# A new order of the pair loop, an earlier first expert transfer, and the first transposed inverse by TensorE's transposes

## The reference

```python
proj = rmsnorm(x) @ w_in                       # 2048 -> 3360 (RWKV) + 4096 (retention)
# RWKV-7, per head and step:
sa = einsum('hvk,hk->hv', S, -kk)
S = S * w + sa[..., None] * b + v[..., None] * k
y = einsum('hvk,hk->hv', S, r)
# then a norm of y per head, a bonus term and a gate
# retention, per head and chunk of 128:
o = ((q @ k.T) * decay) @ v + (q @ R) * decay_q
# then a norm and silu(gate)
x = x + concat(y_a, y_b) @ w_out
x = x + moe(rmsnorm(x))                        # top 1 of 4 groups, top 2 of 8 experts
out = rmsnorm(x)
```

## Time and profile before

| | us |
|---|---|
| median of three runs | 2032.34 |
| the profiled execution's own time | 2036.68 |
| its span | 2034.9 |
| PE busy, share of the span | 1682.4, 83% |
| DVE, ACT, POOL busy | 605.2, 279.8, 124.0 |
| pass 0 | 33.7 to 125 |
| pair loop, seven passes | 125 to 900 |
| drain and output projection | 900 to 1068 |
| logits, routing, first gather | 1068 to 1090 |
| experts and stores | 1090 to 2034.9 |

### The profile page before, as it was taken

One profiled execution on the slowest core, in us unless ns is written; L12 is line 12 of the kernel. 1 busy time (PEld: TensorE's weight loads), 2 busy tenths in 40 slices (PEclk: granted clock), 3 DMA queues, 4 the chain that ended last, 5 costly groups with the idle time before them and its releaser, 6 DMA issues.

```text
span 2034.9 us, 25650 instructions
## 1 busy us (share of the span) xinstructions
PE 1682.4 (83%) x9134; PEld 1020.5 (50%) x9134; DVE 605.2 (30%) x1094; ACT 279.8 (14%) x560; POOL 124.0 (6%) x101
## 2 busy tenths in 40 slices
PE   8998999989998989899999758586685857777665
PEld 4776767767776767676666313232231312323111
DVE  6536264545445363632003101111110101111013
ACT  2221222222221212120103000000000000000002
POOL 0201111020202020110000000000000000000000
PEclk9999999999999999999999878797887878878778
DMA  7223222213222232215616999999999999999996
GB/s 280 99 77 112 72 95 76 92 64 105 82 72 90 77 110 76 94 65 170 273 62 283 427 428 428 427 428 428 429 428 429 428 428 428 429 428 429 427 410 244
DMA packets 71041, 510.35 MB, mean 251 GB/s; under 512 B 20401, under 2 KB 23601, under 8 KB 37585
## 3 DMA queue, kind: packets, MB, share of 16 engines
q1 hardware_dynamic: 70944, 509.60, 62.1%
q0 software_dynamic: 48, 0.12, 0.0%
HBM read 499.87 MB, written 9.82 MB: 250 GB/s over the span
## 4 chain that ended last, share of the span: by engine, by line
PE 52%; DMA 32%; DVE 10%; issue 2%; SPq 1%; ACT 1%; DVEq 1%; ACTq 0%
DMA arena<-w_up 21%; PE ps_PJ L641 16%; DMA arena<-w_down 11%; DVE arena L1302 10%; PE ps_C L960 8%; PE ps_PJ L839 7%; PE ps_C L699 2%; PE ps_C L722 1%; SPq L510 1%; ACT arena L1043 1%; PE ps_C L1011 1%; PE ps_SB L1011 1%; PE ps_YB L1011 1%; PE ps_RT L805 1%; PE ps_SB L756 1%
## 5 line engine op out<-in xcount | busy, mean ns | idle before, releaser
L641 PE MATMUL ps_PJ<-arena 128*128 128x320 f32 x1792 | 542.1, 434 | 4.0 <-ACTq L374 4.0
L960 PE MATMUL ps_C<-arena 128*32 128x512 f32 x2048 | 285.1, 720 | 176.6 <-DMA arena<-w_gate 95.8
L641 PEld LDWEIGHTS ps_PJ<-arena 128*128 128x128 f32 x1792 | 319.8, 190 | 111.5 <-issue 11.6
L960 PEld LDWEIGHTS ps_C<-arena 128*32 128x32 f32 x2048 | 80.9, 129 | 374.7 <-issue 372.4
L1302 DVE TENSOR_TENSOR arena<-arena,ps_PJ 128x512 f32<-128x512 f32 (+2 forms) x112 | 73.5, 657 | 572.8 <-PE ps_PJ L936 449.2
L1043 ACT ACTIVATE arena<-ps_C 128x512 f32<-128x512 f32 (+1 forms) x68 | 40.6, 598 | 1064.9 <-PE ps_C L960 594.4
L1302 DVE TENSOR_TENSOR arena<-arena 128x320 f32<-128x320 f32 (+12 forms) x238 | 161.4, 678 | 47.5 <-ACTq L374 25.8
L1780 POOL TENSOR_TENSOR arena<-arena 128x640 f32<-128x640 f32 (+2 forms) x80 | 118.2, 1478 | 780.5 <-DVEq L374 423.1
L839 PE MATMUL ps_PJ<-arena 128*128 128x320 f32 x512 | 145.8, 437 | 2.1 <-DVEq L374 2.1
L929 PE MATMUL ps_PJ<-arena 128*128 128x128 f32 (+1 forms) x768 | 136.2, 308 | 0.0
L929 PEld LDWEIGHTS ps_PJ<-arena 128*128 128x128 f32 (+1 forms) x768 | 104.4, 188 | 40.8 <-issue 11.7
(11 more groups left out here) (183 smaller groups left out, 1364.0 us busy)
## 6 DMA issues: line engine op xcount, KB each, us to landing
arena<-w_gate SPq DMA_DIRECT2D x64, 2048.0 KB, 20.1
arena<-w_up SPq DMA_DIRECT2D x64, 2048.0 KB, 20.9
arena<-w_down SPq DMA_DIRECT2D x64, 2048.0 KB, 20.8
arena<-win SPq DMA_DIRECT2D x59, 1024.0 KB, 4.8
arena<-w_out SPq DMA_DIRECT2D x16, 1024.0 KB, 6.5
arena<-xT SPq DMA_DIRECT2D x8, 640.0 KB, 6.9
arena<-s_ret SPq DMA_DIRECT2D x8, 512.0 KB, 3.8
o_sret<-arena SPq DMA_DIRECT2D x8, 512.0 KB, 4.0
```

Of the source, the lines that this page charges most:

```text
L641: last = mm(pj(j)[:, 0:T], wt[j % NSLOT][:, kt, :], hT[:, kt, :], start=kt == 0, stop=kt == KT - 1)
L960: last = mm((GB, UB)[u][h * CAP:(h + 1) * CAP, :], xg[:, kt, h * CAP:(h + 1) * CAP], w[h][:, k, :], start=kt == 0, stop=kt == KT - 1)
```

## The change

It has five parts. First, `PLAN` and `PLAN0` are new: the retention steps from `sc` to `ms` move from the pass after into their own pass, steps are cut in smaller ones (`pa` into `p1`, `p2`; `pb` into `b1`, `b2a`, `b2b`; `ss` into `sq`, `ss`; `mu` into `my`, `mu`; `pv` into `pr`, `pw`; `ms` into `ms`, `mr`, `mg`; the rotations in two each), and banks and the drain's fill (`LATE`) are set accordingly. Second, `lp` and `ls` transpose the masked `GM` on TensorE, and ScalarE copies the result into `L`; VectorE's two maskings are gone. Third, a new step `u0` transposes `V` of the four chunks on TensorE, and ScalarE copies it into `U`, in place of GpSimd's two products over 640 columns; GpSimd keeps two of 128 columns for the samples. `V` itself is made in two pieces, `v0` and `v1`. Fourth, in the opening of the experts only the first gather stands ahead of the first matmuls, which work on half of the rows (k 0 to 3); then the second gather follows, and the four weight pieces 8 to 11 are fetched in halves (`ex_half`), the first half as soon as those matmuls are done. Fifth, the last logits come ahead of the last transposes, and a sum moves behind the routing's last product.

```diff
-    "C2": ["g2", "du1", "du2", "du3", "du4", "s0", "s1", "s2", "s3", "mu", "va"],
+    "C2": ["g2", "u0", "du1", "du2", "du3", "du4", "s0", "s1", "s2", "s3"],
...
-    "RT": ["tkk", "tvv", "sc", "rt1", "oo", "rt2", "ms", "u1", "u2"],
+    "RT": ["tkk", "sc", "tvv", "rt1", "oo", "rt2", "ms", "u1", "u2", "mu", "va"],
-WARM = [28, 5]
+WARM = [24, 5]
...
-    "k": "-@g -s0 | zw -tvv | -r1 | za -sc | -a1 pc | -rt1 | -s1 | -oo",
-    "r": "-r2 @k | pe -rt2 | -a2 | -ms | -s2 | ss -u1 | -r3 -u2 | -a3 ps",
-    "v": "@r | -s3 | | | -mu pa | pb | -va |",
-    "q": "@v | g0 pd | g1 | g2 | g3 | lp g4 | ls |",
-    "kr": "@q | z1 | zs1 | d1 ds1 | -pv | z2 rq | zs2 | d2 ds2",
-    "vr": "@kr | z3 | tv d3 | rk tb bs | z4 tk | tkk d4 | ts | z5",
-    "g": "@vr gg | rs0 d5 | rs1 | r0 | as | a0 | us |",
+    "k": "-@g -u1 -th | -s1 -mr | zw -u2 | -r2 za -mg | pc | -a2 pe | | -s2",
+    "r": "@k | -r3 | sq | -a3 ss | p1 | -s3 ps | | b1 b2a",
+    "v": "@r | | b2b | -my | -mu | g4 p2 | g0 | g1",
+    "q": "@v v0 g2 -va | g3 v1 | lp ls | u0 | z1 | zs1 pd | | d1 ds1",
+    "kr": "@q | rqa z2 | zs2 | rqb d2 ds2 | | z3 | tv | d3",
+    "vr": "@kr | rka z4 tb | tk | rkb d4 -pr | ts | z5 | tkk -pw | d5",
+    "g": "@vr r0 sc bs | tvv a0 gg | rs0 | s0 rt1 | rs1 oo | r1 rt2 as | ms | a1 us",
...
-    "r": "-r2 @k | -rt2 | -a2 | -ms | zw -s2 | za pc ss -u1 | pe -r3 -u2 | -a3 ps",
+    "k": "| | | | | | |",
+    "r": "@k | | | sq | zw | za pc | ss pe | p1 ps",
+    "v": "@r b1 | b2a | b2b | | | g4 p2 | g0 | g1",
+LATE = {"u1": 1, "s1": 2, "u2": 1, "r2": 2, "a2": 2, "s2": 2, "r3": 2, "a3": 2, "s3": 4, "mu": 5, "va": 5}
...
+            def ex_half(c, half, arrived):
+                s = ESLOT[c % NSLOT_C]
+                dst = arena[:, experts_at + s * BIGSLOT:experts_at + (s + 1) * BIGSLOT].rearrange("p (k n) -> p k n", k=8)
+                src = w_gate[c % QUAD, 2 * F:4 * F, :].rearrange("(p k) n -> p k n", k=8)
+                sp.dma_start(dst[:, 4 * half:4 * half + 4, :], src[:, 4 * half:4 * half + 4, :]).then_inc(arrived, 16)
...
-            for c in range(NSLOT_C, PIECES):
+            sp.wait_ge(sem("half_used"), 1)
+            for c in range(NSLOT_C, NSLOT_C + QUAD):
+                ex_half(c, 0, sem("half_in"))
+            for c in range(NSLOT_C, NSLOT_C + QUAD):
+                sp.wait_ge(ex_used, c - NSLOT_C + 1)
+                ex_half(c, 1, ex_in[ESLOT[c % NSLOT_C]])
...
+                    wait_freed(pe, "g2", p)
+                    wait_freed(pe, "g3", p)
                     for c in range(NC):
-                        last = mm(b[:, c * P:(c + 1) * P], AR[:, c, 0:P], Bd[:, c, :], start=True, stop=True)
+                        last = nc.tensor.transpose(b[:, c * P:(c + 1) * P], GM[:, c, 0:P], ident)
+                    last.then_inc(full(s), 1)
+                elif s == "u0":
+                    wait_done(pe, "inv0v", p)
+                    for c in range(NC):
+                        last = nc.tensor.transpose(b[:, c * P:(c + 1) * P], V[:, c, :], ident)
                     last.then_inc(full(s), 1)
                 elif s == "ls":
-                    mm(b[:, 0:P], AR[:, NC, 0:P], Bd[:, NC, :], start=True, stop=True).then_inc(full(s), 1)
+                    nc.tensor.transpose(b[:, 0:P], GM[:, NC, 0:P], ident).then_inc(full(s), 1)
                 elif s in ("tv", "tb", "tk"):
                     src = {"tv": Vd, "tb": Bd, "tk": Kd_}[s]
...
-                        gather(2 * q + 1, sel0)
-                    pe.wait_ge(named["xg_done"], 4 * it + (4 * q + 2 if opening else 2 * q + 2))
+                        if q == 1:
+                            gather(2 * q + 1, sel0)
+                            if first(it):
+                                pe.wait_ge(sem("half_in"), 16 * QUAD)
+                    if opening and q == 0:
+                        pe.wait_ge(named["xg_done"], 4 * it + 1)
+                    else:
+                        pe.wait_ge(named["xg_done"], 4 * it + (4 * q + 2 if opening else 2 * q + 2))
...
+                            if opening and q + u == 0 and k == 4:
+                                last.then_inc(sem("half_used"), 1)
+                                gather(1, sel0)
+                                pe.wait_ge(named["xg_done"], 4 * it + 2)
...
+                elif s == "lp":
+                    wait_filled(act, s, p)
+                    if not first(p):
+                        act.wait_ge(lmk, 5 * p)
+                    A(L[:, 0:NC, :], bank(s)[:, :].rearrange("p (c n) -> p c n", c=NC), ACT.Copy).then_inc(free(s), 1)
+                elif s == "u0":
+                    wait_filled(act, s, p)
+                    A(U[:, 0:NC, :], bank(s)[:, :].rearrange("p (c n) -> p c n", c=NC), ACT.Copy).then_inc(free(s), 1)
+                elif s == "ls":
+                    wait_filled(act, s, p)
+                    A(L[:, NC, :], bank(s)[:, 0:P], ACT.Copy).then_inc(free(s), 1)
...
+                elif s == "b1":
+                    if not first(p):
+                        wait_filled(dve, "ts", p - 1)
+                    by_heads(Bd, lambda o, h: STT(o, heads(t1)[h], 0.5, heads(ei)[h], ALU.mult, ALU.mult))
+                    by_heads(Kd_, lambda o, h: TT(o, heads(kp)[h], heads(ei)[h], ALU.mult))
+                elif s == "b2a":
                     if not first(p):
                         dve.wait_ge(full("y"), p)
                     by_heads(AR, lambda o, h: STT(o, heads(kn)[h], -1.0, heads(e0)[h], ALU.mult, ALU.mult))
-                    TT(AR[:, :, P:192], heads(xm["r"]), heads(e1), ALU.mult)
-                    by_heads(Bd, lambda o, h: STT(o, heads(t1)[h], 0.5, heads(ei)[h], ALU.mult, ALU.mult))
-                    by_heads(Kd_, lambda o, h: TT(o, heads(kp)[h], heads(ei)[h], ALU.mult)).then_inc(done("bd"), 1)
+                elif s == "b2b":
+                    TT(AR[:, :, P:192], heads(xm["r"]), heads(e1), ALU.mult).then_inc(done("bd"), 1)
                 elif s == "bs":
...
-                elif s == "lp":
-                    wait_filled(dve, s, p)
-                    if not first(p):
-                        dve.wait_ge(lmk, 5 * p)
-                    TT(L[:, 0:NC, :], bank(s)[:, :].rearrange("p (c n) -> p c n", c=NC), lmask[0][:, None, :].broadcast_to([P, NC, P]), ALU.mult).then_inc(free(s), 1)
-                elif s == "ls":
-                    wait_filled(dve, s, p)
-                    TT(L[:, NC, :], bank(s)[:, 0:P], lmask[1], ALU.mult).then_inc(free(s), 1)
-                    wait_freed(dve, "g4", p)
-                    TT(V[:, :, :], GM[:, :, 0:P], m0T[:, None, :].broadcast_to([P, NCH, P]), ALU.mult)
-                    TT(V[:, :, :], V[:, :, :], ident[:, None, :].broadcast_to([P, NCH, P]), ALU.add).then_inc(done("inv0v"), 1)
+                elif s in ("v0", "v1"):
+                    cs = slice(0, 2) if s == "v0" else slice(2, NCH)
+                    nch = cs.stop - cs.start
+                    TT(V[:, cs, :], GM[:, cs, 0:P], m0T[:, None, :].broadcast_to([P, nch, P]), ALU.mult)
+                    last = TT(V[:, cs, :], V[:, cs, :], ident[:, None, :].broadcast_to([P, nch, P]), ALU.add)
+                    if s == "v1":
+                        last.then_inc(done("inv0v"), 1)
...
-                    TT(U[:, :, :], L[:, :, :], lvl[0][:, None, :].broadcast_to([P, NCH, P]), ALU.mult)
-                    TT(U[:, :, :], U[:, :, :], ident[:, None, :].broadcast_to([P, NCH, P]), ALU.add).then_inc(done("inv0u"), 1)
+                    TT(U[:, NC, :], L[:, NC, :], lvl[0], ALU.mult)
+                    TT(U[:, NC, :], U[:, NC, :], ident, ALU.add).then_inc(done("inv0u"), 1)
```

85 lines of the change are left out of this document (50 added, 35 removed), and 2 rows, old and new, of the table BANKS.

## The result

The changed kernel takes **1987.29 us** (median of 4 runs, 1986.59 to 1988.96) against 2032.51 us (2032.01 to 2033.68, 4 runs) beside it: a ratio of 0.9771, 95% interval 0.9759 to 0.9783. It mattered in the opening (e6, e9).

A forecast was written before the change was run, and what follows sets the result against it. TensorE's work bounds the loop, the weight stream the experts. Loop -28, pass 0 +5.8, drain +1, opening -8 sum to -29.2: from 2036.68 to 2007.5, median 4.3 lower, 2003 us; range 1988 to 2022.

The forecast's parts named there:

- the chain up to the first refill: Everything before the first refill (1099 us): one chain on TensorE, where a microsecond saved is a microsecond of the result.
- `v0` and `v1` at their lower bound: VectorE's products of V in the loop: 2.1 us, no longer beside GpSimd, where 4.3 was the upper end.
- the opening's logits: Opening of the experts: earlier last logits, four fewer warming matmuls and the moved sum together give -1.5 us.
- the stream's length: Expert weights from the first refill on: bound by the stream at 425 GB/s, so an earlier start ends equally earlier.
- The rival of the cooling clock: Pair loop: ten more transposes a pass drop the clock to 1.2 GHz, 3.9 us a pass more, about 2034; chance 0.02.
- What a wait costs: TensorE in the loop: about 0.1 us of refilling behind each wait; fewer waits give -0.3 us a pass.
- The new waits: TensorE in a pass: `mu` 1.9, `lp` 0.7, `z1` 0.5, small ones 0.4; 3.5 us in place of 7.16.
- The title's part: `u0` replacing GpSimd's large products on U: worth what it takes from `z1` and VectorE, about 1 us a pass.
- The opening: Start of the experts: first halves asked for at 1090.1, not 1098.91; less 0.8 at `w_down`, taken as -8 us.
- Pass 0: First pass: loses 5.8 us, waits of 8.9 against 3.1, of which 7.3 before `g4`.
- The drain: After the loop: `a2` and `s2` wait about 0.7 and 1.1 against one wait of 0.6; +1 us.
- TensorE's work is all that is left: Rival, loop: VectorE and GpSimd keep up, 2 to 3 us more a pass, 1983 to 1992; chance 0.14.

The follow-up runs named there:

- e6: Changed kernel with the gathers' last operand 64 rows high again in place of 128: 1990.43 us, ratio 0.9780 to the kernel before.
- e9: Kernel before with only the gathers' last operand 128 rows high in place of 64, rows above 64 zero-filled: 2032.59 us, ratio 0.9986.
- e2: Changed kernel with `mu` moved two projection parts back, behind `g4` and `p2`: 1973.26 us, ratio 0.9701 to the kernel before.
- e8: Changed kernel with `mu` two parts later, `v0` behind `g3`, `u0` one later; in pass 0 `ps` before `p1`, `g4` one later: 1965.50 us, ratio 0.9651.
- e1: Changed kernel without `u0` and its ScalarE copy; GpSimd makes all of U by two products of 640 columns again: 1987.21 us, ratio 0.9765.
- e4: Kernel before, old order, with only `u0` (four transposes of V on TensorE, ScalarE copy; GpSimd keeps the small chunk): 2031.81 us, ratio 0.9984.
- e3: Changed kernel with `ps` ahead of `p1` in pass 0: 1984.33 us, ratio 0.9750 to the kernel before.

## Why the prediction was wrong

**Right in kind**: what bounds the kernel, the chain up to the first refill, which waits would be new and on whom, `v0` and `v1` at their lower bound, the opening's logits (-1.5), and the stream's length. The rival of the cooling clock is out for the loop: with nine more transposes a pass (the prediction says ten) the period's granted clock is still 1.00.

**What a wait costs: the step that failed, with the size of the new waits.** "Each wait also costs about 0.1 us of refilling behind it; with fewer waits, -0.3" was mis-sized, in the price and in the count. e2 took away 1.66 and gave 1.89; e8's lp took 0.55 and gave 0.77. So a wait costs its idle time and 0.22 to 0.23 more. The rows show it on both sides: the three parts ahead of the old wait before `mu` take 3.40 us where their pace is 3.23, and `mu` behind it 0.78 where the same product takes 0.70 without a wait (`va`). The prediction counted the second only. Outside its waits TensorE's time in a period fell by 1.57; `lp`, `ls` and `u0` are 0.17 of that, which leaves 1.4 where I had 0.3: 1.1 a pass, 7.7 us in all. Five waits fewer at 0.23 make 1.15 of the 1.4; the other 0.25 lies in gaps too short to be listed as waits, and was not tried by itself.

The Trainium skill, page TensorE: Matmul & The Clock Gate, section "Single matmul latency", gives a single bfloat16 matmul a constant of 398 cycles at 2.4 GHz besides its columns; an estimate from it is 0.17 us for a pipeline that must drain once. The two experiments, in float32, give somewhat more.

**The new waits**, nearly as large an error: 2.44 for 3.5 a pass, 7.4 us in all. `mu` 1.66 (1.9), `lp` 0.55 (0.7), `z1` 0.23 (0.4 to 0.5), the small ones none (0.4). The walk was right in its order; the gaps per handover were put a little high, and I added 0.4 for waits that I had not walked.

**The title's part** is worth nothing in the new order (e1) and 0.57 a pass in the old one (e4), not "about 1 us a pass". What freed VectorE's products from GpSimd is the order: `v0` and `v1` stand ahead of `lp`, on which GpSimd waits. The 2.15 us a product of 640 columns beside GpSimd, 1.60 (3.20 for two) with part of that overlap, and 0.45 and 0.58 for products of 256 and 384 columns without it (1.02 for the 640 together) agree with the exclusive lock of the Trainium skill's page SBUF — State Buffer (section "SBUF: two separate sides").

**The opening**: -12.0 for -8. One term was missing: the 128-row operand. It took 1.4 from the gather ahead of the first matmuls, and 0.8 at `w_down` did not arise (e6). The sixteen matmuls took 3.64, not 5.6, because they ran at a granted clock of 1.00, where I had taken the pace of the old ones at 0.57. No edit is shown to bring that: the clock is 1.00 there with the narrow gather of e6 and with the two of e4 in the old opening as well, and 0.57 in the trace of the kernel before only. So some 2 of the 12.0 us are luck of that one trace. They cancel the 1.8 lost behind the drain, where the same trace had the cheap case.

**Pass 0** cost +5.65 for the +5.8 of the prediction, and that is luck. Its waits grew from 3.08 to 7.12 us, 4.0 and not 5.8: `g4` waited 6.51 for 7.3, `lp` and `z1` 0.6 for 1.2, and the small ones nothing. About 2 us were the low clock behind the wait of 6.51, which no term stood for.

**The drain** cost 0.15 and not 1: `a2` and `s2` waited 0.5 and 0.6 in place of one wait of 0.6. **The output projection** started slow: +1.8, not foreseen.

In sum, against the forecast, by the two traces: refill -7.7, waits -7.4, rest of the loop -0.5, pass 0 and drain -1.0, opening -4.0, the clock behind the drain +1.8: -18.8. The median of 1987.3 lies 15.7 below the forecast of 2003; the 3 us between the two are single executions against medians. The two profiled ones are 50.1 apart, 48.0 up to the first request and 2.1 behind it (the clock in the tail, below); the medians are 45.2 apart, for the profiled one of before lay 4.2 above its median and that of the changed kernel 0.7 below. Where the other executions were quicker or slower no trace shows. The rival "TensorE's work is all that is left" (1983 to 1992, chance 0.14) named the right time, partly by luck, with half of the mechanism: three waits are left, and e8 shows that 2.66 us a pass more were to be had.

## What to carry to other kernels

Count waits as well as their length: on the engine that bounds this loop each one cost nearly a quarter of a microsecond beyond its idle time, so that two short waits are worse than one of the same sum. Before a step is given to another engine, look at what its consumer waits for last; if that is still the same, nothing is gained, as in e1. Read a diff for shapes too: a wider operand in one call was worth 3.2 us between two traces (e6), as much as the swap of two steps in pass 0 (e3).
